# LayerNorm ends of a two-block transformer: the second centring moved from VectorE to GpSimd, scale and scaled slices placed in PSUM banks

## The reference, cut to what matters

```
def layer_norm(x, g, b):
    xf = x.astype(jnp.float32)
    mu = jnp.mean(xf, axis=-1, keepdims=True)
    var = jnp.mean(jnp.square(xf - mu), axis=-1, keepdims=True)
    return ((xf - mu) * lax.rsqrt(var + EPS) * g + b).astype(x.dtype)

def second_block(x, ...):
    h = layer_norm(x, ln_in_g, ln_in_b)
    for l in range(2):
        h = layer_norm(DN_ALPHA * h + token_mixers(h, ...), ln1_g[l], ln1_b[l])
        h = layer_norm(DN_ALPHA * h + conv_ffn(h, ...), ln2_g[l], ln2_b[l])
    return h
```

## Time and profile before

| | before |
|---|---|
| median of three runs | 2589.61 us |
| lowest and highest run | 2587.82, 2592.54 us |
| the profiled execution's own time | 2590.14 us |
| its span in the trace | 2588.2 us |
| PE busy | 2481.5 us (96%) |
| DVE busy | 1719.8 us (66%) |
| ACT busy | 1024.9 us (40%) |
| POOL busy | 958.2 us (37%) |
| chain that ended last | PE 78%, DVE 9%, issue 6%, ACT 3%, POOL 2% |

### The profile page before, as it was taken

The page is one execution under the profiler, slowest core; times in us unless marked ns, Lnnn a source line. Parts: engine busy times, 40 slices in busy tenths (PEclk is TensorE's granted clock), DMA queues, the critical chain, the costliest instruction groups (busy, mean ns, idle before and its releaser), DMA issues.

```text
span 2588.2 us, 33451 instructions
## 1 busy us (share of the span) xinstructions
PE 2481.5 (96%) x11222; PEld 1907.6 (74%) x11222; DVE 1719.8 (66%) x2281; ACT 1024.9 (40%) x1623; POOL 958.2 (37%) x391
## 2 busy tenths in 40 slices
PE   7999999999999999999899889999989988999997
PEld 5676787888777688888676467788767746778876
DVE  7654774587777777276787667718668755781875
ACT  4444432232344532123554644313345454431333
POOL 2222444444310044444263034444435403453452
PEclk9999999999999999999999999999999999999999
DMA  5212232232332223223222022322322202232222
GB/s 171 78 58 61 86 97 90 89 100 95 102 92 74 74 89 101 90 94 106 67 90 62 13 66 85 105 86 89 104 77 83 66 8 74 81 98 89 94 97 77
DMA packets 65342, 217.48 MB, mean 84 GB/s; under 512 B 8416, under 2 KB 8672, under 8 KB 65120
## 3 DMA queue, kind: packets, MB, share of 16 engines
q1 hardware_dynamic: 64384, 214.79, 25.8%
q10 hardware_dynamic: 864, 1.44, 0.2%
HBM read 207.81 MB, written 2.10 MB: 81 GB/s over the span
## 4 chain that ended last, share of the span: by engine, by line
PE 78%; DVE 9%; issue 6%; ACT 3%; POOL 2%; DMA 0%; DVEq 0%; SPq 0%; ACTq 0%; POOLq 0%
PE bank_G L668 23%; PE bank_G L670 23%; PE bank_G L669 23%; POOL wlo L559 2%; DVE conv_up L1105 2%; DVE prod L1125 1%; ACT whi L639 1%; DVE h L952 1%; PE bank_S L1705 1%; PE bank_S L2221 1%; PE bank_X L1733 1%; PE bank_O L1957 1%; PE bank_O L1719 1%; PE bank_S L1946 1%; DVE conv_up L1104 1%
## 5 line engine op out<-in xcount | busy, mean ns | idle before, releaser
L559 POOL TENSOR_TENSOR wlo<-raw,whi 128x1024 fp32r<-128x1024 f32 (+2 forms) x361 | 905.3, 2509 | 1518.1 <-ACT whi L639 1493.0
L668 PE MATMUL bank_G<-n_hi,whi 128*128 128x512 f32 x2248 | 903.8, 402 | 49.3 <-DVE n_lo L956 27.2
L669 PE MATMUL bank_G<-n_lo,whi 128*128 128x512 f32 x2248 | 880.9, 392 | 0.0
L670 PE MATMUL bank_G<-n_hi,wlo 128*128 128x512 f32 x2248 | 880.8, 392 | 0.0
L639 ACT ACTIVATE whi<-raw 128x1024 fp32r<-128x1024 f32 (+2 forms) x389 | 403.4, 1038 | 603.8 <-PE bank_G L670 603.6
L668 PEld LDWEIGHTS bank_G<-n_hi,whi 128*128 128x128 f32 x2248 | 425.3, 189 | 168.7 <-DVE n_lo L956 36.3
L670 PEld LDWEIGHTS bank_G<-n_hi,wlo 128*128 128x128 f32 x2248 | 425.3, 189 | 91.3
L669 PEld LDWEIGHTS bank_G<-n_lo,whi 128*128 128x128 f32 x2248 | 425.9, 189 | 88.2 <-issue 4.8
L668 PE MATMUL bank_G<-a_hi,whi 128*128 128x512 f32 x704 | 277.9, 395 | 9.1 <-DVE a_lo L1127 3.9
L669 PE MATMUL bank_G<-a_lo,whi 128*128 128x512 f32 x704 | 275.2, 391 | 0.0
L670 PE MATMUL bank_G<-a_hi,wlo 128*128 128x512 f32 x704 | 275.0, 391 | 0.0
(11 more groups left out here) (333 smaller groups left out, 2681.9 us busy)
## 6 DMA issues: line engine op xcount, KB each, us to landing
raw<-in_w_mix_in SPq DMA_DIRECT2D x40, 512.0 KB, 3.3
raw<-in_w_hyb_in SPq DMA_DIRECT2D x25, 512.0 KB, 3.4
raw<-in_w_diff_in SPq DMA_DIRECT2D x24, 512.0 KB, 3.3
raw<-in_w_up0a SPq DMA_DIRECT2D x22, 512.0 KB, 3.3
raw<-in_w_up0b SPq DMA_DIRECT2D x22, 512.0 KB, 3.3
raw<-in_w_up1a SPq DMA_DIRECT2D x22, 512.0 KB, 3.3
raw<-in_w_up1b SPq DMA_DIRECT2D x22, 512.0 KB, 3.3
raw<-in_w_up2a SPq DMA_DIRECT2D x22, 512.0 KB, 3.3
```

Of the source, the lines that this page charges most:

```text
L559: pool.tensor_tensor(b.wlo[:, g.slot, w], b.raw[:, g.slot, w], b.whi[:, g.slot, w], ALU.subtract).then_inc(b.lo_ready, 1)
L668: pe.matmul(out, b.whi[:, g.slot, w], hi[:, hi_at + k, :], start=(k == 0), stop=False)
L669: pe.matmul(out, b.whi[:, g.slot, w], lo[:, lo_at + k, :], start=False, stop=False)
L670: mm = pe.matmul(out, b.wlo[:, g.slot, w], hi[:, hi_at + k, :], start=False, stop=(k == pieces - 1))
```

## The change

POOL takes over the centring of all eight slices of each norm, now with a mean that ACT first copies from O[0] to SBUF (`b.mean`). ACT writes the scale into S[0] instead of `rstd`. DVE scales from h into one of four banks in turn (X[0], X[1], O[1], S[1]), and the low part, `n_hi` and the biased h are made from that bank. A bank is used again after four slices, so that DVE waits from k = 4 on until ACT has made the biased h of slice k-4. The centring stands in POOL's program ahead of `ramp_lo`'s two halves, for norm 4 at the very end.

```diff
@@ ramp_lo @@
     g = Index(FIRST[name] + 2)
+    norm_centre_pool(pool, b, NORMS[n])
     pool.wait_ge(b.half_hi, n + 1)
@@ new functions @@
+def normed_bank(b, k):
+    return (b.X[:, 0, :], b.X[:, 1, :], b.O[:, 1, :], b.S[:, 1, :])[k % 4]
+
+def norm_centre_pool(pool, b, x):
+    pool.wait_ge(b.mean_taken, x.n + 1)
+    for k in range(KD):
+        h = b.h[:, k, :]
+        pool.wait_ge(b.shift_squared, 8 * x.n + k + 1)
+        pool.tensor_tensor(h, h, b.mean[:, :], ALU.subtract).then_inc(b.centred, 1)
@@ norm_end_act @@
     act.wait_ge(b.first_moment, n + 1)
+    act.activation(b.mean[:, :], b.O[:, 0, :], ACT.Copy, scale=1.0 / D).then_inc(b.mean_taken, 1)
     act.activation(b.acc[:, :], b.O[:, 0, :], ACT.Square, scale=1.0 / D).then_inc(b.moment_squared, 1)
...
-    act.activation(b.rstd[:, :], b.rstd[:, :], ACT.Exp, scale=-0.5).then_inc(b.scale_ready, 1)
+    act.activation(b.S[:, 0, :], b.rstd[:, :], ACT.Exp, scale=-0.5).then_inc(b.scale_ready, 1)
...
-        act.activation(b.h[:, k, :], b.h[:, k, :], ACT.Identity, bias=v_(b, x.bias, k)).then_inc(b.h_ready, 1)
+        act.activation(b.h[:, k, :], normed_bank(b, k), ACT.Identity, bias=v_(b, x.bias, k)).then_inc(b.h_ready, 1)
...
-            act.activation(b.n_hi[:, k, :], b.h[:, k, :], ACT.Identity, bias=v_(b, x.bias, k)).then_inc(b.nhi_ready, 1)
+            act.activation(b.n_hi[:, k, :], normed_bank(b, k), ACT.Identity, bias=v_(b, x.bias, k)).then_inc(b.nhi_ready, 1)
@@ norm_end_dve @@
-    def centre(k):
-        dve.scalar_tensor_tensor(h[k], b.O[:, 0, :], -1.0 / D, h[k], ALU.mult, ALU.add).then_inc(b.centred, 1)
     def low(k):
         dve.wait_ge(b.nhi_ready, x.nhi + k + 1)
-        dve.scalar_tensor_tensor(b.n_lo[:, k, :], h[k], v_(b, x.bias, k), b.n_hi[:, k, :], ALU.add,
+        dve.scalar_tensor_tensor(b.n_lo[:, k, :], normed_bank(b, k), v_(b, x.bias, k), b.n_hi[:, k, :], ALU.add,
                                  ALU.subtract).then_inc(b.nlo_ready, 1)
...
-    for k in range(AHEAD[0]):
-        centre(k)
...
-    for k in range(*AHEAD):
-        centre(k)
     dve.wait_ge(b.scale_ready, 2 * n + 2)
     for k in range(KD):
         dve.wait_ge(b.centred, 8 * n + k + 1)
-        dve.scalar_tensor_tensor(h[k], h[k], v_(b, x.gain, k), b.rstd[:, :], ALU.mult, ALU.mult).then_inc(b.normed, 1)
-        if k + AHEAD[1] < KD:
-            centre(k + AHEAD[1])
+        if k >= 4:
+            dve.wait_ge(b.h_ready, 8 * n + k - 3)
+        dve.scalar_tensor_tensor(normed_bank(b, k), h[k], v_(b, x.gain, k), b.S[:, 0, :], ALU.mult,
+                                 ALU.mult).then_inc(b.normed, 1)
         if x.split and k:
             low(k - 1)
@@ POOL's program, at its end @@
+            norm_centre_pool(pool, b, NORMS[4])
```

More of the change, by code:

```diff
@@ L350, in allocate @@
     b.centred = sem("centred")
+    b.mean_taken = sem("mean_taken")
     b.normed = sem("normed")
@@ L942, in norm_tile_dve @@
         add(total, total, square_at(b, x, 6), "q6", "q5", squared=7)
-AHEAD = (1, 4)
 def norm_end_dve(dve, b, x):
     n, h = x.n, [b.h[:, k, :] for k in range(KD)]
-    def centre(k):
-        dve.scalar_tensor_tensor(h[k], b.O[:, 0, :], -1.0 / D, h[k], ALU.mult, ALU.add).then_inc(b.centred, 1)
     def low(k):
         dve.wait_ge(b.nhi_ready, x.nhi + k + 1)
-        dve.scalar_tensor_tensor(b.n_lo[:, k, :], h[k], v_(b, x.bias, k), b.n_hi[:, k, :], ALU.add,
+        dve.scalar_tensor_tensor(b.n_lo[:, k, :], normed_bank(b, k), v_(b, x.bias, k), b.n_hi[:, k, :], ALU.add,
                                  ALU.subtract).then_inc(b.nlo_ready, 1)
```

## The result

| | before | changed |
|---|---|---|
| median of the runs | 2589.90 us (4 runs, 2587.82 to 2592.54) | 2573.18 us (4 runs, 2572.45 to 2574.53) |
| profiled execution, own time | 2590.14 us | 2574.53 us |
| its span, mean granted clock | 2588.2 us, 0.985 | 2572.6 us, 0.988 |

The ratio is 0.9949, 95% interval 0.9927 to 0.9972: faster by 13.2 us, give or take 5.8; the two medians of the table differ by 16.7 us, which lies inside that interval. Timed again beside other kernels the changed one had 2573.68 us (6 runs, 2572.69 to 2575.41) against 2588.52 us (11 runs, 2582.67 to 2591.39), ratio 0.9947 [0.9935, 0.9958].

A forecast was written before the change was run, and what follows sets the result against it. PE was taken as the bound, with DVE pacing each norm up to slice 2. Chain 3.8, starts 0.9 and ramps 7.6, less 0.2 for norm 4, gave 12.1 us off: 2577.5 us, range 2573.5 to 2584.

The forecast's parts named there:

- The bound: Whole kernel: PE is busy nearly throughout, so time is won only where it stands still or runs slowly.
- DVE's chain: Scaling to first low part in each norm: 1.57 us instead of 2.52, so 0.95 us earlier; then 1.32 us a slice.
- The start: Start of scaling after the mean: 0.27 us earlier in norms 1 to 3, 0.10 us in norm 0.
- What PSUM costs DVE: Scale and scaled slices in PSUM: no extra DVE time; by the skill's rule some 0.6 us in all.
- POOL stays ahead: POOL's centring at 1.30 us a slice keeps ahead of DVE's scaling, with 3.4 us to spare before the third tile.
- The ramp: PE's restart to 49th matmul, norms 0 to 3: 13.2 us instead of 15.1, with 11 slow matmuls; 1.9 us less each.
- rival A: Ramps behind the norms: low clock lasts 7.3 us as before, each ramp only 0.8 us less; 2582 us, chance 0.20.
- Norm 4: Kernel's end, with no PE behind it: POOL's centring sets the pace and it comes 0.2 us later.
- The sum: Chain 3.8, starts 0.9, ramps 7.6, less 0.2 for the last norm: 12.1 us less, median 2577.5 us.
- B: Norms: POOL's centrings and DVE instructions shut each other out, 1.98 us a pair; about 2614 us, slower, chance 0.04.
- C: Third tile or later stages: gain lost again as the 2 us of cover is gone; 2586 to 2590 us, chance 0.08.
- D: Norms 1 and 3: POOL's centring paces the slices, needing over 1.5 us each; part of the range, no chance of its own.

The follow-up runs named there:

- run with the term in a bank: Changed kernel with the second term of norm 0's variance written to PSUM bank X[1] instead of SBUF: 2572.19 us.
- place-only run: Kernel before with the scale in S[0] and the scaled slices in the four PSUM banks, DVE still centring: 2586.67 us, ratio to before 1.0003.
- pause run: Changed kernel, except that PE waits for the low part of slice 2 before it multiplies slice 1: 2582.64 us, ratio to before 0.9986.

## Why the prediction was right, point by point

The mechanism held: DVE's shorter chain brings the restart forward, PE's waits for slices 1 and 2 go, and the low clock is shorter. The total came out near the measured one also because single terms were off in both directions: against the forecast the starts gave 0.7 us less and the ramps 0.2, the chain gave 0.2 more and norm 4 0.4.

**The bound**: right. PE is busy for 96% as before, and what changed is its pause and its slow clock.

**DVE's chain, 0.95 us a norm**: right. The first low part stands 1.51 us behind the scaling (forecast 1.57; 2.52 before), so 1.01 us earlier; slices are 1.32 apart, as forecast.

**The start, 0.27 in norms 1 to 3 and 0.10 in norm 0**: 0.41, 0.18 and 0.41 measured, but in norm 0 the scaling came 0.78 us later (5.13 instead of 4.35). This term of the sum was mis-sized: 0.9 us forecast in the four norms, 0.2 measured. I named L970 as having the bad form and 1.3 us as the worst, and still put the gain at 0.10; it ran into POOL's centring and took 1.66 us instead of 0.69 (the run with the term in a bank shows the whole 0.98 us). POOL was centring there, as it had started 1.4 us ahead of that instruction (1269.91 and 1271.27), right behind ACT's copy; by the prediction's own times the two had to meet, so a case close to the worst was the likely one.

**What PSUM costs DVE: nothing**: right. 0.75 us a scaling against 0.74, and starts 0.66 apart in both. The Trainium skill's access overheads (Perfetto Trace Analysis, Optimizing Scalar/DVE Operations), by which I had estimated some 0.6 us in all, don't show here, nor in the place-only run. Exp into PSUM took 0.60 us, the lower of its bounds.

**POOL stays ahead at 1.30 us a slice**: right; it took 1.24 us (1.29 in norm 0). The cover of the third tile held: POOL waited 3.84 us for ACT's half there, and no wait of PE took its place.

**The ramp, 15.1 to 13.2 us, 1.9 each**: right in sum, 7.4 measured for 7.6 (restart to 49th: 15.15, 15.13, 15.70 and 14.58 before, 12.69, 13.23, 13.75 and 13.50 now). Its parts were right too: 8, 10, 13 and 12 slow matmuls, in the mean 10.8, against the 11 that I took; behind the restart the low clock lasted 3.6, 4.7, 5.8 and 5.3 us, in the mean 4.8. That the middle between two rows of other stages met this mean so closely is in part luck, since the single norms spread over most of the range between them. But rival A's arithmetic was off: it gave the 15.1 us 16.5 slow matmuls, where norm 1 counts 14 and the rest was the two waits, 1.2 us. Those waits go whatever the clock does, so A, with its slow matmuls unchanged, should have stood at 2580 (14 slow ones give a ramp of 13.9, 1.3 less each), not 2582.

**Norm 4, 0.2 us later**: wrong in sign. POOL does pace it, as this DVE row of the changed kernel shows, but at 1.23 us a slice, 9.82 for eight, so that it ends 0.2 earlier.

```profile
2565.02 0.75 DVE L985 SCALAR_TENSOR_TENSOR bank_X<-h,vec,bank_S 128x512 f32<-128x512 f32 x1 [0.47 <-POOL h L873]
```

**The sum**: 12.1 us forecast, 11.8 shown in the changed places. The median fell by 13 to 17 us depending on the pair, which leaves 1 to 5 us that the sum doesn't hold. In the two profiled executions the 3.8 us outside the norms stand beside 27.3 and 23.9 us of low clock there. The place-only version has the DVE chain of before, and its profiled execution had 6.2 us less in "the rest" and 4.2 us less slow clock: the kernel before itself varies by that much. The profiled execution of before, against which the sum was made, stood high in both columns. By the last table such differences go with the low clock in code that didn't change, and half of the 3.8 us is explained by it (one stretch of 3.4 us more). What makes the clock fall there in one execution and not in another stays open.

**The rivals.** A fell to the pause run; B's mutual slowing exists, with 1.67 us an instruction, and showed for two whole SBUF inputs alone; C's cover held; D showed only in norm 4.

## What to carry to other kernels

Work moved from DVE to GpSimd beside a busy DVE paid here only with at most one whole SBUF input in each DVE instruction that ran meanwhile (2573 us against 2602); look at every instruction in that stretch, the one-off ones too, and put an operand in PSUM. Where PE restarts into work that arrives in slices, slices that arrive faster than PE takes them can pay twice, once in the waits and once in the slow clock, whereas an earlier start alone can be partly given back (0.98 us at the restart of norm 0 gave 0.50 at the 49th matmul). Make the sum from the places that change, and compare several executions of the kernel before wherever its clock differs between them. One thing wasn't run: the kernel before with the low part of slice 0 moved ahead of the centrings, so how much of the 8.6 us another order on DVE alone would have given isn't known.
